# Opening units, squares and gates of a two-block transformer kernel, and the place of GLA's decays, rearranged

## What is computed

```python
h = rmsnorm(x, norm_mix_g)                  # x * rsqrt(mean(x*x) + EPS) * g
q_m, k_m, v_m, if_pre, o_pre, ... = split(h @ w_in)
qk = silu(causal_depthwise_conv(concat(q_m, k_m), conv_w, conv_b))
ig, lf = if_pre[:4] + b, log_sigmoid(if_pre[4:] + b)
hm = mlstm_cell(q_m, k_m, v_m, ig, lf)
y_a = sigmoid(o_pre) * norm(hm)
...
log_a = log_sigmoid(a_lr @ w_alpha2 + b_alpha) / GLA_TAU
b = cumsum(log_a)                            # per chunk of 64
qe, ke, kd = q * exp(b), k * exp(-b), k * exp(b_last - b)
```

## Time and profile before

| | |
|---|---|
| median of 3 runs | 2023.84 us (2021.43 to 2025.13) |
| profiled execution, its own time | 2025.35 us |
| its span, first to last instruction | 2023.6 us |
| mean granted PE clock | 0.985 of full speed |
| PE, DVE, ACT, POOL busy | 97%, 52%, 31%, 14% |

### The profile page before, as it was taken

The page is one execution under the profiler, slowest core; times in us unless marked ns, Lnnn a source line. Parts: engine busy times, 40 slices in busy tenths (PEclk is TensorE's granted clock), DMA queues, the critical chain, the costliest instruction groups (busy, mean ns, idle before and its releaser), DMA issues.

```text
span 2023.6 us, 23620 instructions
## 1 busy us (share of the span) xinstructions
PE 1963.2 (97%) x9642; PEld 1592.5 (79%) x9642; DVE 1044.8 (52%) x1456; ACT 634.5 (31%) x1053; POOL 284.6 (14%) x181
## 2 busy tenths in 40 slices
PE   6999999999999999999999999999999999999997
PEld 5788888888887888888888777877777878888885
DVE  6666633344455744344344765656676544344344
ACT  4333322233333432232234322224444333223221
POOL 3121220011111111010013000111111131011012
PEclk9999999999999999999999899999999989999998
DMA  4222223232311322322323111321121313323222
GB/s 160 72 69 79 76 92 107 93 94 73 88 58 48 120 94 94 104 94 96 96 89 97 63 63 63 104 73 63 53 63 37 120 53 104 96 96 100 94 87 70
DMA packets 52444, 171.87 MB, mean 85 GB/s; under 512 B 5879, under 2 KB 9279, under 8 KB 52336
## 3 DMA queue, kind: packets, MB, share of 16 engines
q1 hardware_dynamic: 51616, 169.21, 26.3%
q10 hardware_dynamic: 720, 1.15, 0.2%
HBM read 168.12 MB, written 2.21 MB: 84 GB/s over the span
## 4 chain that ended last, share of the span: by engine, by line
PE 87%; DVE 9%; ACT 3%; issue 1%; POOL 1%; DMA 0%; DVEq 0%; ACTq 0%; POOLq 0%
PE PS L1008 25%; PE PS L1010 25%; PE PS L1009 25%; PE PS L1112 1%; PE PS L1311 1%; PE PS L1127 1%; PE PS L1289 1%; DVE WL L1648 1%; PE PS L1333 1%; PE PS L1150 1%; PE PS L1073 1%; PE PS L1159 1%; PE PS L1173 1%; DVE AR L1676 1%; ACT WH L1376 1%
## 5 line engine op out<-in xcount | busy, mean ns | idle before, releaser
L1008 PE MATMUL PS<-HH,WH 128*128 128x512 f32 x1368 | 541.7, 396 | 14.1 <-DVE WL L1648 10.8
L1010 PE MATMUL PS<-HH,WL 128*128 128x512 f32 x1368 | 535.6, 392 | 0.0
L1009 PE MATMUL PS<-HL,WH 128*128 128x512 f32 x1368 | 535.2, 391 | 0.0
L1376 ACT ACTIVATE WH<-RAW 128x1024 fp32r<-128x1024 f32 (+2 forms) x320 | 326.0, 1019 | 405.7 <-PE PS L1010 405.6
L1648 DVE TENSOR_TENSOR WL<-RAW,WH 128x1024 fp32r<-128x1024 f32 (+2 forms) x257 | 318.7, 1240 | 234.6 <-ACT WH L1376 232.8
L1008 PE MATMUL PS<-AH,WH 128*128 128x512 f32 x1096 | 435.2, 397 | 2.3 <-DVE WL L1648 1.8
L1010 PE MATMUL PS<-AH,WL 128*128 128x512 f32 x1096 | 430.0, 392 | 0.0
L1009 PE MATMUL PS<-AL,WH 128*128 128x512 f32 x1096 | 429.8, 392 | 0.0
L1008 PEld LDWEIGHTS PS<-HH,WH 128*128 128x128 f32 x1368 | 258.7, 189 | 70.2 <-DVE WL L1648 10.8
L1010 PEld LDWEIGHTS PS<-HH,WL 128*128 128x128 f32 x1368 | 258.3, 189 | 54.7
L1009 PEld LDWEIGHTS PS<-HL,WH 128*128 128x128 f32 x1368 | 258.8, 189 | 52.1
(11 more groups left out here) (238 smaller groups left out, 1423.7 us busy)
## 6 DMA issues: line engine op xcount, KB each, us to landing
RAW<-wst SPq DMA_DIRECT2D x288, 512.0 KB, 3.4
RAW<-wst SPq DMA_DIRECT2D x16, 384.0 KB, 3.0
RAW<-wst SPq DMA_DIRECT2D x16, 256.0 KB, 2.5
XT<-xT SPq DMA_DIRECT2D x3, 512.0 KB, 7.8
AR<-scr SPq DMA_DIRECT2D x16, 64.0 KB, 4.1
AR<-scr SPq DMA_DIRECT2D x8, 128.0 KB, 4.7
AR<-w SPq DMA_DIRECT2D x2, 512.0 KB, 3.8
out<-XT SPq DMA_DIRECT2D x4, 256.0 KB, 2.0
```

The source lines that it names most:

```text
L1008: T.matmul(out, wh, XH[:, k, :], start=k == 0, stop=False)
L1009: T.matmul(out, wh, XL[:, k, :], start=False, stop=False)
L1010: m = T.matmul(out, wl, XH[:, k, :], start=False, stop=k == nk - 1)
L1376: t = A.activation(WH[:, i % NW, 0:n], RAW[:, i % NR, 0:n], ACT.Copy, scale=1.0)
```

## The change

Units om0 and om1 move from head 1 to places 7 and 8, ahead of `mlstm_scores(0)`; head 0 then fills with six units instead of eight. In the opening ACT splits unit 0 right after tile 0, unit 1 after tile 1, and squares follow in groups; it also runs a tiny Copy first, on data that DVE sets. Each square has its own buffer, DVE adds them, POOL's `start` is gone, and DVE makes the WL of unit 1. The constants come in two DMAs: ident and mean from ACT's queue, the rest last on SP's. `lead_first` takes the place of `lead` for the first three units: unit 0 is evicted before the last quarter of unit 2, `gates_1` is issued between the two convolutions, and `gates_2` in unit 3. Token turns are held back until `mlstm_scores(0)`. In GLA the step 0 of decays 1 to 3 is put in `later`, so each step runs one flush later. Left out below: the sizes of the constants' table ("mean" becomes one column), and the new semaphore's declaration.

```diff
...
@@ -73,8 +73,10 @@
                 add(n, 4 * g + hp)
     head(0, {1: ("if", 0, 0, 8)})
+    add("om", 0)
+    add("om", 1)
     for h in range(3):
-        head(h + 1, {0: ("om", 2 * h, 0, 8), 3: ("om", 2 * h + 1, 0, 8)})
+        head(h + 1, {0: ("om", 2 * h, 0, 8), 3: ("om", 2 * h + 1, 0, 8)} if h else {})
     add("om", 6)
     add("om", 7)
     pair(0)
@@ -119,6 +121,11 @@
 OB = 5
 NSA_PARTS = [(0, (0, 1)), (3, (0,)), (3, (1,)), (2, (0,)), (2, (1,)), (1, (0, 1))]
+
+
+def lo_on_pool(i):
+
+    return i % 2 == 1 and i > 1 and UNITS[i][0] in BUSY_DVE
 def unit_of(name, j=0, k0=0):
@@ -303,9 +310,9 @@
         e.products(i, range(6))
     else:
         e.products(i, range(nk // 2))
-        flush(e)
+        flush(e, not e.turns_apart)
         e.products(i, range(nk // 2, nk))
-    flush(e)
+    flush(e, not e.turns_apart)
     evict(e, i)
@@ -383,39 +390,64 @@
     evict(e, d)
+def lead_first(e):
+
+    for i in range(3):
+        e.sum_bank("sum", i)
+    ahead(e, 0)
+    for k in range(0, 8, 2):
+        e.products(0, range(k, k + 2))
+        e.products(1, range(k, k + 2))
+    e.products(2, range(0, 2))
+    e.turn_bank("fold", "n1")
+    e.fold("n1")
+    ahead(e, 1)
+    e.products(2, range(2, 6))
+    e.turn_bank("spread", "n1")
+    e.spread("n1")
+    ahead(e, 2)
+    evict(e, 0)
+    e.products(2, range(6, 8))
+
+
 def mlstm(e):
-    lead(e, 0, "n1", False)
+    e.turns_apart = True
+    lead_first(e)
     e.ones()
+    e.gates_1()
+    flush_all(e)
+    evict(e, 1)
     quarter(e, 3, 0)
-    e.gates_1()
+    e.gates_2()
     for q in (1, 2, 3):
         quarter(e, 3, q)
     evict(e, 3)
-    e.gates_2()
-    for g in range(3):
-        unit(e, 4 + g)
-        e.turn_bank("vector", g)
-        e.bias_vector(g)
+    for i in range(4, 9):
+        unit(e, i)
+        if i < 7:
+            e.turn_bank("vector", i - 4)
+            e.bias_vector(i - 4)
     e.store_vectors()
+    e.turns_apart = False
     e.turn_bank("columns")
     e.gate_columns()
     e.ring = [0, 1]
-    at = 7
+    at = 9
     for h in range(4):
-        n = 8 if h < 3 else 11
+        n = (6, 8, 8, 11)[h]
         fill = Fill(e, range(at, at + n), 1)
         at += n
         mlstm_scores(e, h)
         fill.quarters(4)
         e.weights(h)
-        fill.quarters(12)
+        fill.quarters(12 if h else 8)
         for t in range(4):
             e.hold((*SB, OB)[t], "numer", h, t)
         e.numerators(h)
         fill.quarters(6)
         e.normed(h)
         e.turns_apart = h < 3
-        fill.quarters(10 if h < 3 else 6)
+        fill.quarters(4 * n - 22 if 0 < h < 3 else 6)
         if h == 3:
             mlstm_scores(e, 4)
         fill.drain(h == 3)
@@ -552,8 +584,7 @@
     for n, j in GLA_FIRST[3:]:
         unit(e, unit_of(n, j))
         if n == "gk":
-            e.decay(1, 0)
-            e.later.append(("decay", 1, 1))
+            e.later.append(("decay", 1, 0))
     e.ring = [0, 1]
     for h in range(4):
         gla_turned(e, h)
@@ -566,8 +597,7 @@
         units(e, GLA_UNITS[h][1][:1])
         e.gla_scaled(h)
         if h < 2:
-            e.decay(h + 2, 0)
-            e.later.append(("decay", h + 2, 1))
+            e.later.append(("decay", h + 2, 0))
         if h == 0:
             e.later.append(("final", 0, 1))
         if h == 3:
@@ -854,7 +885,7 @@
         OT2 = part(0, 4096).rearrange("p (j t) -> p j t", j=8)
         F2 = parts(5632, *[512] * 6)
-        SUMS = {"n1": parts(14336, 512, 512, 512), "n2": [SS0[:, 0:512], SS0[:, 512:1024], SS1[:, 0:512]],
+        SUMS = {"n1": parts(13836, *[512] * 8), "n2": [SS0[:, 0:512], SS0[:, 512:1024], SS1[:, 0:512]],
                 "n3": parts(0, 512, 512, 512), "n4": parts(1536, 512, 512, 512), "post2": parts(0, 512, 512, 512),
                 "fpost2": parts(4096, 512, 512, 512)}
         TMP = {"post2": parts(nsa_at + 8192, 512, 512), "fpost2": parts(8704, 512, 512)}
@@ -907,6 +938,8 @@
             return 0 if b else 128
         def sums(name, n):
+            if name == "n1":
+                return SUMS[name][n]
             a, b, acc = SUMS[name]
             return acc if n == 0 else (a, b)[n % 2]
@@ -932,13 +965,15 @@
                 for g, (j, n) in enumerate(((0, 1), (1, 1), (2, 2), (4, 2), (6, 2))):
                     d = S.dma_start(XT[:, j:j + n, :], xT_d[:, j:j + n, :])
                     d.then_inc(*x_in[g].next("x", g))
-                    if g < 3:
+                    if g < 2:
                         s.load(g)
-                S.dma_start(C[:, :], con_d).then_inc(*con_in.next("con"))
+                s.load(2)
                 S.dma_start(tab[0:32, :], relb_d).then_inc(*table_in.next("tab"))
                 S.dma_start(oh[0:33, :], oh_d).then_inc(*table_in.next("oh"))
                 s.load(3)
                 s.load(4)
+                n = CON["big"]
+                S.dma_start(C[:, n:NCON], con_d[:, n:NCON]).then_inc(*con_rest_in.next("con_rest"))
             def load(s, i):
                 name, j, k0, nk = UNITS[i]
@@ -1096,6 +1131,7 @@
                 b = s.bank["max", h]
                 s.free("max", h)
                 pe.wait_ge(*at("gate_M"))
+                pe.wait_ge(*at("con_rest"))
                 t = T.matmul(PS[:, b, :], con("sel", 128 * h, 128 * h + 128, 0, 4), r1, start=True, stop=True)
                 t.then_inc(*pe_done["mlstm"].next("max_spread", h))
@@ -1349,21 +1385,25 @@
             def start(s):
                 A.dma_start(COL[:, :], col_d).then_inc(*col_in.next("col"))
+                A.dma_start(C[:, 0:CON["big"]], con_d[:, 0:CON["big"]]).then_inc(*con_in.next("con"))
+                act.wait_ge(*at("awake"))
+                A.activation(RC[:, 13:14], RC[:, 12:13], ACT.Copy, scale=1.0)
                 act.wait_ge(*at("col"))
-                for j in range(8):
-                    act.wait_ge(*at("x", (0, 1, 2, 2, 3, 3, 4, 4)[j]))
-                    s.scaled_hi("h1", HH, j, XT[:, j, :], col("mix_g", j))
-                    s.square("n1", j, XT[:, j, :])
-                    if j in (1, 3):
-                        s.split(j // 2)
-                act.wait_ge(*at("con"))
+                for js in ((0,), (1,), (2, 3), (4, 5, 6, 7)):
+                    for j in js:
+                        act.wait_ge(*at("x", (0, 1, 2, 2, 3, 3, 4, 4)[j]))
+                        s.scaled_hi("h1", HH, j, XT[:, j, :], col("mix_g", j))
+                    if js[0] < 2:
+                        s.split(js[0])
+                    for j in js:
+                        s.square("n1", j, XT[:, j, :])
             def scaled_hi(s, x, X, j, src, g):
                 t = A.activation(X[:, j, :], src, ACT.Copy, scale=g)
                 t.then_inc(*act_done["norm"].next(x, "hi", j))
             def square(s, norm, n, src, scale=1.0):
-                if n > 2:
+                if n > 2 and norm != "n1":
                     act.wait_ge(*at("acc", norm, n - 2))
                 t = A.activation(sums(norm, n), src, ACT.Square, scale=scale)
                 t.then_inc(*act_done["norm"].next("sq", norm, n))
@@ -1617,15 +1657,22 @@
             def start(s):
+                V.memset(RC[:, 12:13], 0.0).then_inc(*dve_done["norm"].next("awake"))
                 dve.wait_ge(*at("col"))
                 V.tensor_tensor(GG, COL[:, COLS["final_g"]:COLS["final_g"] + 8], GG, ALU.mult).then_inc(
                     *dve_done["norm"].next("gg"))
                 for j in range(8):
                     dve.wait_ge(*at("x", (0, 1, 2, 2, 3, 3, 4, 4)[j]))
                     s.scaled_lo("h1", HH, HL, j, XT[:, j, :], col("mix_g", j))
-                    if j in (1, 3):
-                        s.split(j // 2)
-                dve.wait_ge(*at("con"))
+                    if j < 2:
+                        s.split(j)
+                    elif j % 2:
+                        for n in (j - 2, j - 1):
+                            dve.wait_ge(*at("sq", "n1", n))
+                            if n > 1:
+                                dve.wait_ge(*at("acc", "n1", n - 1))
+                            t = V.tensor_tensor(sums("n1", 0), sums("n1", 0), sums("n1", n), ALU.add)
+                            t.then_inc(*dve_done["norm"].next("acc", "n1", n))
                 V.memset(xc[:, 0:4], 0.0).then_inc(*dve_done["mlstm"].next("conv_start"))
             def scaled_lo(s, x, XH, XL, j, src, g):
@@ -1641,7 +1688,7 @@
             def split(s, i):
                 n = UNITS[i][3] * 128
-                if i % 2 and UNITS[i][0] in BUSY_DVE:
+                if lo_on_pool(i):
                     return
                 dve.wait_ge(*at("raw", i))
                 dve.wait_ge(*at("hi", i))
@@ -1878,6 +1925,7 @@
             def spread_max(s, h):
                 big = con("big")
+                dve.wait_ge(*at("con_rest"))
                 dve.wait_ge(*at("free", "max", h))
                 V.tensor_tensor(heads_of(Md), heads_of(Mb),
```

(9 more changed lines are left out.)

9 lines of the change are left out of this document (5 added, 4 removed).

## The result

The changed kernel takes **2014.47 us** (median of 4 runs, 2012.64 to 2014.84), against 2024.49 us for the kernel before in the same comparison (2021.43 to 2027.36): ratio 0.9946, 95% interval 0.9932 to 0.9959. It is 10.0 us faster; the forecast was 2015.1, in a range of 2009 to 2021. The profiled execution of the changed kernel took 2014.84 us, its span is 2013.0, which is 10.5 us less than before.

What follows compares the result with a forecast made beforehand. PE is busy 97% of the span, so only its idle or lower-clock time can be won. 4.3 us (opening) + 4.4 (GLA) = 8.7 off 2025.35 gives 2016.65 profiled, median 2015.1; range 2009 to 2021.

Steps and rivals of the forecast that it cites:

- Part 1: Opening: PE's first matmul starts at 8.05 instead of 10.75 us, -2.7 us.
- Part 2: Opening, units 1 and 2: PE's second gap goes as POOL stops adding, -2.7 us; unit 2 ends at 29.5.
- Part 3: Units 3 to 8: 1.9 us given back; gaps of 4.7 and 3.1 us at units 5 and 6, 10.6 loss with slow clock.
- Part 4: Head 0: no change (0), though it loses 10.9 us of cover; bounds -1.7 to +3 us.
- bound -1.7: Head 0: 1.7 us gained if the scores' 3.4 us at a clock of 0.55 come back at full speed.
- bound of +3: Head 0: 3 us lost if the convolutions of units 9 and 10, now back to back, delay DVE.
- Part 5: GLA: deferred decay steps let weight splits go earlier and shrink PE's waits, -4.4 us, bounds 1 and 6.
- a GLA wait that grows: GLA: one of the signs the prediction named as showing it wrong; no size given.
- (a): Units 3 to 8: rival that the chain is shorter and both gaps halve, 2009.2 us; chance 0.17.
- (b): Unit 8 and head 0: rival that the gain is given back in waits behind convolutions, 2023.2 us; chance 0.19.
- (c): Units 4 to 8: rival that PE waits at every weight split, slower at 2029.5 us; chance 0.06.
- (d): Opening: rival that early weights come late, PE starts at 9.3, 2018.1 us; chance within the forecast's 0.58.

Runs made afterwards that it cites:

- weights_late: Changed kernel with ACT's opening in its old order (units 0 and 1's weights behind the second and fourth tile), sums still on DVE: 2017.17 us, ratio 0.996.
- split5_early: Changed kernel with unit 5's weights split right behind `lead_first`, ahead of the gates: 2014.23 us, ratio 0.9951.
- om_back: Changed kernel with om0 and om1 back in head 1 and the opening ending with unit 6 again: 2016.94 us, ratio 0.9968.

## Why the prediction was right

**Part 1, first matmul: -2.7 forecast, -2.3 measured** (8.49 against 10.75; ten experiments with this start have it at 8.15 to 8.40). The walk had the first weights at 5.7, and so they came in most traces; in this one ACT sat idle for 0.56 us until they landed, and WH began at 6.05. HH was late too (4.76, 0.72 us long), but had ended before the weights came, so it cost nothing.

**Part 2: right in kind.** The second gap is gone, HL is at 0.75 and below. Unit 2's end, read from its last six matmuls, is about 30.2: 5.5 us ahead of 35.7, where I took 6.2 and gave 30.3 as the late bound. Twelve matmuls ran at half speed, near the 13 of that bound. But this trace is the latest of ten with the same code: they end unit 2 between 28.7 and 30.2, which is as wide as the forecast's bounds (28.7 and 30.3), with the middle at 29.8. So 29.5 was a fair choice, and how much of it comes true is luck in each trace. Of the gain, weights_late shows that the early weights carry 2.5 us at maxima 3; the share of POOL's absence stays open (0.9 or nothing).

**Part 3: the sum right, its parts shifted.** Gap at unit 5 4.92 (4.7 forecast), at unit 6 2.15 (3.1), half-speed matmuls ten and eight, each 0.2 us longer than at full speed: 2.0 and 1.6 (2.0 and 0.8). That is 10.7 against 10.6. The order of events was the forecast's, about 0.8 us later: Exp began at 38.70 (37.9) and tanh at 42.67 (41.9); WH 5 was done at 44.25 (43.4), POOL's WL at 46.73 (45.9), conv 1 at 49.3 (48.8), WL 6 at 57.5 (57.2). The second gap is the smaller because PE came there at 55.4, not 54.1. What it lacked is that the bank of unit 1 was nearly as late as the weights: "bank 1 being free by then" (41.2) is wrong, since it came free at 44.75, as split5_early shows too (4.1 us of wait on it with the weights ready). It cost nothing in the sum, since the two overlap, but who had built on part 3's text to repair unit 5 would have won nothing. Maxima 0 came at 77.27, not 75.8: 0.7 from part 2, and 0.8 in the six units, which took 5.59 us each beside gaps and slow clock, not 5.46. The lead at that point is 80.7 - 77.27 = 3.4, where the forecast had 4.9; its net of 4.3 had the 0.6 of the later token turn taken off, and by the same count the measured net is 2.8.

**Part 4: head 0 gave 1.2 us, forecast 0, bound -1.7, and head 1 took 0.9 back, forecast nothing.** The sixteen scores took 4.58 us, against 6.28 before: the bound's 1.7 in full, and the token turn that moved into head 0 takes the rest. om_back beside the other experiments shows what holds the scores at the higher clock: the two om units ahead of them. PE does not wait inside head 0; weights(0) ended 5.4 us ahead of PE's numerators, as worked out (92.83 + 1.68, and 99.96). At maxima 1 the changed kernel is 4.7 us ahead, and at maxima 2 (181.11 and 177.32) only 3.8, against 4.3. What it lost stands at head 1's first score: DVE's SiLU product (L1847) is late, and head 1 takes 56.1 us, with 0.57 of wait, where the kernel before and om_back take 55.2 and 55.3 for the same matmuls. So the convolutions behind a shorter head 0 were late after all, but for the next head's scores, where the forecast's bound of +3 did not look.

**Part 5: GLA -4.4 forecast, -5.6 measured**, within the bounds 1 and 6. The two waits of head 1 left 1.7 (1.9 forecast) and the L1759 wait became 1.8 (1.6). Head by head, the gain is 0.3 us up to the scores of head 0 (0.6 forecast at gk0), 0.7 to head 1 and 4.7 to head 2. In that last stretch PE is idle 2.9 us less (3.1 forecast in parts, 1.5 and 1.6) and the same matmuls take 1.8 us less (44.03 and 42.19). The term that was mis-sized is the clock: I counted back half of 1.4 us, and all of it and more came back, since nothing in that stretch runs at the lower clock any more. Another 1.4 us of clock came back up to head 0's scores, where the new wait took most of it. Over the whole stretch the forecast was 3.7 idle and 0.7 clock, and measured are 2.3 and 3.4: the sum is near because two errors oppose each other. And the forecast's own sign of being wrong, a GLA wait that grows, is there: the token turn's, 0.6 to 1.2, and a new one of 1.1.

**The table loads.** By the Trainium skill (ScalarE: Activation LUTs, What ACT_TABLE_LOAD costs) each switch would have had a drain of about 1.4 us beside its load, and by an estimate from that page the gap at unit 5 would have been 2.8 us longer. The trace disagrees: 0.63, 1.28, 0.72 and 1.28 make 3.91 of the 3.97 us from Exp to tanh, which leaves no room for a drain. The rows were the right source.

**The rivals.** (a) fell on its own terms: both gaps were there. (b) needed PE to wait inside head 0 and behind unit 8; it did neither, but the same mechanism cost 0.9 us in head 1. (c) needed 23.3 us of loss in units 3 to 9, and there were 10.7. (d) had the first matmul at 9.3; it was 8.49.

**Luck.** For the profiled execution the forecast was 2016.65, and it took 2014.84, 1.8 us less: the opening fell 0.5 short, GLA came 1.2 over, and 1.0 us more lies at the end of the span, where no edit is. The median agrees better (2015.1 and 2014.47) only because the changed kernel's profiled execution lay 0.4 us above its median, where the forecast took over the 1.5 of the kernel before. The forecast's own bounds were added up loosely as well: the 2.7 in "2011 (1.7 + 2.7)" has no row, and part 5's bounds would give 1.6 on that side and 3.4 on the other. The result lies so near the middle that this did not matter.

## What to carry to other kernels

When a wait is removed, walk each engine's queue to the next one, and ask of the next waiting instruction for everything that it needs, not for the last thing alone: here the later weights hid the bank, and one alone gave nothing that could be measured; both together, with the next units' weights also placed in another engine's idle time, gave 9.9 us at head 0. Filling work ahead of a dense stretch can be worth more than the gap it covers: in om_back a gap of 2.2 us came with scores that took 7.0 us instead of 4.6. And a tenth of a per cent in the total can be the clock at a far place, so compare start times of the same instruction before a cause is given, and take more than one trace of the same code to see how far these differ by themselves (up to 1.1 us at head 0 here).
